# Two-block network on one core: gate projection inside the attention stage, semaphore clears outside a Block, and the first expert pieces loaded during routing

## The reference

```
h = rms_norm(x);  proj = h @ w_in          # 1024 x 7168
lru_in, lru_gate, q, k, v, g_lru, g_attn = split(proj)   # 7 parts of 1024 columns
y_lru  = (gelu(lru_gate) * rg_lru(conv(lru_in))) @ w_lru_o
y_attn = diff_attention(q, k, v) @ w_attn_o   # 8 heads, two maps each, causal by chunks of 64
x = x + (sigmoid(g_lru) * y_lru + sigmoid(g_attn) * y_attn) @ w_out
x = x + cross_attention(x, mem);  x = x + two_level_moe(rms_norm(x))
```

## Time and profile before

| | |
|---|---|
| median of 3 runs | 4880.08 us (4880.0 to 4886.49) |
| profiled execution | 4875.11 us, its span 4873.3 us |
| TensorE busy | 4016.8 us, 82% of the span |
| granted TensorE clock, mean | 0.906 |
| proj_g stage | about 3075 to 3262 us |
| attention stage | about 3267 to 3587 us |
| routing of the first expert layer | about 1754 to 1842 us |

### The profile page before, as it was taken

How to read it: one execution, slowest core, us unless ns; L and a number is a source line. 1 busy time by engine, 2 the same in 40 slices (tenths; PEclk the granted TensorE clock), 3 DMA queues, 4 the chain that set the end, 5 groups by cost and what they waited for, 6 DMA issues and landing times. The chain is left out here.

```text
span 4873.3 us, 76497 instructions
## 1 busy us (share of the span) xinstructions
PE 4016.8 (82%) x31217; PEld 3213.4 (66%) x31217; DVE 2769.6 (57%) x4050; ACT 2034.3 (42%) x3437; POOL 470.9 (10%) x376
## 2 busy tenths in 40 slices
PE   6999877868887747999859888777779896499994
PEld 4888654448886526888748666665668655288883
DVE  4222154666654667999741675216652445399995
ACT  3111023645443315777531444116641333277772
POOL 0000012210001200111010231000000000111111
PEclk8999977979998878999969999889989898699997
DMA  5332212652223418999642333231112313699996
GB/s 198 130 135 95 105 64 63 188 149 78 80 75 126 142 71 356 389 398 390 260 160 86 99 110 103 95 118 40 40 57 82 112 52 128 252 402 411 412 412 250
DMA packets 368225, 842.35 MB, mean 173 GB/s; under 512 B 32207, under 2 KB 241135, under 8 KB 317446
## 3 DMA queue, kind: packets, MB, share of 16 engines
q1 hardware_dynamic: 349790, 787.43, 43.8%
q0 software_dynamic: 12032, 41.96, 2.7%
q10 hardware_dynamic: 6056, 8.08, 0.5%
HBM read 673.03 MB, written 164.35 MB: 172 GB/s over the span
## 5 line engine op out<-in xcount | busy, mean ns | idle before, releaser
L504 PE MATMUL psum<-proj_hi,proj_w 128*128 128x512 f32 (+2 forms) x1728 | 462.0, 356 | 15.4 <-DVE proj_w L546 13.8
L2719 DVE TENSOR_TENSOR moe_lo<-moe_raw,moe_hi 128x2048 fp32r<-128x2048 f32 x192 | 436.4, 2288 | 45.2 <-ACT moe_hi L2667 45.1
L4346 DVE TENSOR_TENSOR moe_lo<-moe_raw,moe_hi 128x2048 fp32r<-128x2048 f32 x192 | 428.2, 2284 | 33.7 <-ACT moe_hi L4301 33.7
L2667 ACT ACTIVATE moe_hi<-moe_raw 128x2048 fp32r<-128x2048 f32 x192 | 367.8, 1919 | 136.9 <-PE psum L2620 136.8
L4301 ACT ACTIVATE moe_hi<-moe_raw 128x2048 fp32r<-128x2048 f32 x192 | 356.9, 1910 | 41.5 <-PE psum L4262 41.5
L504 PEld LDWEIGHTS psum<-proj_hi,proj_w 128*128 128x128 f32 (+1 forms) x1728 | 304.1, 188 | 69.0 <-DVE proj_w L546 14.2
L504 PE MATMUL psum<-proj_lo,proj_w 128*128 128x512 f32 (+2 forms) x864 | 306.4, 355 | 0.0
L515 DVE COPY proj_out<-psum 128x512 f32<-128x512 f32 (+3 forms) x54 | 32.5, 602 | 355.3 <-PE psum L504 355.3
L1796 DVE COPY_PREDICATED chunks_X<-chunks_msk,psum 128x128 f32<-128x128 int32 x400 | 107.8, 301 | 161.5 <-PE psum L1549 137.3
L1709 ACT ACTIVATE chunks_T<-psum 128x128 f32<-128x128 f32 x400 | 103.1, 277 | 216.0 <-PE psum L1539 211.0
L504 PE MATMUL psum<-h_hi,proj_g_w 128*128 128x512 f32 x512 | 159.9, 394 | 29.2 <-DVE proj_g_w L546 29.2
(11 more groups left out here) (634 smaller groups left out, 9690.1 us busy)
## 6 DMA issues: line engine op xcount, KB each, us to landing
moe_raw<-in_w_down SPq DMA_DIRECT2D x128, 1024.0 KB, 8.1
moe_raw<-in_w_gate_up SPq DMA_DIRECT2D x128, 1024.0 KB, 10.3
moe_raw<-in_w_gate SPq DMA_DIRECT2D x64, 1024.0 KB, 9.0
moe_raw<-in_w_up SPq DMA_DIRECT2D x64, 1024.0 KB, 10.0
uT<-proj_out SPq DMA_DIRECT2D x35, 640.0 KB, 3.0
chunks_pr<-prim SPq DMA_DIRECT2D x40, 512.0 KB, 4.1
proj_raw<-in_w_in SPq DMA_DIRECT2D x17, 1024.0 KB, 7.8
hT<-in_w_mod SPq DMA_DIRECT2D x32, 512.0 KB, 4.7
```

The costliest lines, as they stand in the source:

```text
L504: ins = nc.tensor.matmul(bank[e * nch + c][0:width, 0:n], l, r, start=(k == 0 and i == 0), stop=(k == KD - 1 and i == 2))
L2667: nc.scalar.activation(hi[:, n % R], raw[:, n % RAW], ACT.Copy).then_inc(s["hi_ready"], 1)
L2719: nc.vector.tensor_tensor(lo[:, n % R], raw[:, n % RAW], hi[:, n % R], ALU.subtract).then_inc(s["lo_ready"], 1)
L4346: nc.vector.tensor_tensor(lo[:, n % R], raw[:, n % RAW], hi[:, n % R], ALU.subtract).then_inc(s["lo_ready"], 1)
```

## The change

Three things change.

1. **Semaphore clears.** The exit of a Stage no longer opens a Block: GpSimd gets the clears directly after the stage's last barrier. The other engines go on. The semaphores stay reserved until the next exit.
2. **First pieces.** The eight ring slots of moe1 (four pieces of w_gate, four of w_up of expert 0) are loaded in route1, behind the router's weights and ahead of the clearing of acc. Their room is what mix's input took, and a new tile.
3. **Gates.** The stage proj_g and the stage branches are gone. The 768 gate matmuls become 32 units of 24, one in each wide step of attention: half of a unit ahead of turn(j-1), half behind it, into bank 7. ACT splits 16 weight tiles (gate_leading), DVE makes their rests (gate_rest), ACT empties each unit (gate_out), and SP loads 16 tiles of 512 KB and stores 32 results of 256 KB within attention. columns_of moves to bank 5 and to steps i = 0 to 3. gT is loaded in mixed, in eight DMAs of 512 KB, of which four stand ahead of the second weight tile. gemm_rows takes h_hi and h_lo as room for its weights, with the same instructions.

```diff
     def __exit__(self, *exc):
-        if exc[0] is None:
-            with self.nc.Block() as block:
-                @block.gpsimd
-                def _(pool):
-                    for s in self.sems:
-                        pool.sem_clear(s)
+        if self.sems:
+            if Stage.retired is not None:
+                Stage.retired.close()
+            for s in self.sems:
+                self.nc.gpsimd.sem_clear(s)
+            Stage.retired = self.sem_ctx
...
@@ route1, SP
                 sp.dma_start(wr[:, :, :], w_router.rearrange("(k p) e -> p k e", p=P)).then_inc(w_in, 16)
+                for n in range(ahead.RAW):
+                    sp.dma_start(ahead.raw(n), ahead.rows(w_gate if n < 4 else w_up, 0, n % 4)).then_inc(ahead.raw_in[n], 16)
                 sp.wait_ge(zeroed, 1)
...
@@ experts1, SP
                 def load(n, src):
-                    if n >= RAW:
-                        sp.wait_ge(s["lo_ready"], n - RAW + 1)
-                    sp.dma_start(raw[:, n % RAW], src).then_inc(raw_in[n % RAW], 16)
+                    if n < RAW:
+                        return
+                    sp.wait_ge(s["lo_ready"], n - RAW + 1)
+                    sp.dma_start(raw(n), src).then_inc(raw_in[n % RAW], 16)
...
@@ diff_attention
-        STATS, GROUPS_AT = PAIR + 2, PAIR + 4
+        STATS, GROUPS_AT = PAIR + 2, PAIR + NT
...
+                load_g(0)
+                load_g(1)
+                for u in range(2 * TILES_G):
+                    if u % 4 == 0 and 2 <= u // 4 + 1 < HEADS2:
+                        sp.wait_ge(s["o_mm"], NT * (u // 4))
+                        load(u // 4 + 1)
+                    if u % 2 == 0:
+                        load_g(u // 2 + 2)
+                    c, b = u // 2, u % 2
+                    sp.wait_ge(s["g_ev"], u + 1)
+                    sp.dma_start(gates[c * P:(c + 1) * P, b * BANK:(b + 1) * BANK], g_out[:, u % 4, :]).then_inc(g_stored[u % 4], 16)
...
+                def gate_unit(u, part):
+
+                    c, b = u // 2, u % 2
+                    if part == 0:
+                        pe.wait_ge(s["g_lo"], c + 1)
+                        if u:
+                            pe.wait_ge(s["g_ev"], u)
+                    for k in range(4 * part, 4 * part + 4):
+                        for i, (l, r) in enumerate(((0, 0), (1, 0), (0, 1))):
+                            ins = nc.tensor.matmul(bank[7][:, :], g_w[:, c % 2, l, k, :], h_part[r][:, k, b * BANK:(b + 1) * BANK],
+                                                   start=(k == 0 and i == 0), stop=(k == KD - 1 and i == 2))
+                    if part == 1:
+                        ins.then_inc(s["g_mm"], 1)
...
+                    u = unit_at(j)
+                    if u is not None:
+                        gate_unit(u, 0)
                     if 1 <= j <= J:
                         turn(j - 1)
+                    if u is not None:
+                        gate_unit(u, 1)
                     if 2 <= j <= J + 1:
                         values(j - 2)
...
@@ attention, ACT
+                def gate_leading(c):
+                    act.wait_ge(g_in[c % 2], 16 * (c // 2 + 1))
+                    if c >= 2:
+                        act.wait_ge(s["g_mm"], 2 * (c - 1))
+                    nc.scalar.activation(g_w[:, c % 2, 0, :, :], g_raw[:, c % 2], ACT.Copy).then_inc(s["g_hi"], 1)
+
+                def gate_out(u):
+                    act.wait_ge(s["g_mm"], u + 1)
+                    if u >= 4:
+                        act.wait_ge(g_stored[u % 4], 16 * (u // 4))
+                    nc.scalar.activation(g_out[:, u % 4, :], bank[7][:, :], ACT.Copy).then_inc(s["g_ev"], 1)
+
+                gate_leading(0)
                 act.wait_ge(s["lam"], 1)
...
@@ mixed_T
                 load(0)
-                load(1)
+                for k in range(KD):
+                    sp.dma_start(act_T[0][:, k, :], lru[k * P:(k + 1) * P, :]).then_inc(lru_in[k], 16)
+                    if k == 3:
+                        load(1)
```

More of the change, by code:

```diff
@@ L2431, in _, with __init__, raw, rows @@
                                 .then_inc(lo_ready, 1)
-def route1(nc, bank, cst, hT, w_router, acc, idx, gates):
+class Ahead1:
+    RAW = 8
+    def __init__(self, nc, hold, room):
+        self.first = room[:, :, :].rearrange("p (r k) n -> p r k n", k=2)
+        self.second = hold.enter_context(nc.sbuf_tensor("ahead1_raw", [P, self.RAW // 2, 2, D], F32))
+        self.raw_in = [nc.alloc_semaphore(f"ahead1_raw_in{i}") for i in range(self.RAW)]
+    def raw(self, n):
+        n, half = n % self.RAW, self.RAW // 2
+        return self.first[:, n] if n < half else self.second[:, n - half]
+    @staticmethod
+    def rows(m, e, j):
+        return m[e, 2 * j * P:2 * (j + 1) * P, :].rearrange("(p k) n -> p k n", k=2)
+def route1(nc, bank, cst, hT, w_router, acc, idx, gates, ahead, w_gate, w_up):
     with Stage(nc, "route1") as st:
@@ L2516, in _, with experts1 @@
                 nc.vector.tensor_copy(idx[:, E1:E1 + 1], bank[5][:, E1:E1 + 1]).then_inc(fin, 1)
[L2519 to L2525 removed]
+def experts1(nc, bank, cst, h2, w_gate, w_up, w_down, acc, idx, gates, xs_in, added, ahead, room):
+    RAW, R = ahead.RAW, 4
     with Stage(nc, "moe1") as st:
[L2527 removed]
+        raw, raw_in, rows = ahead.raw, ahead.raw_in, ahead.rows
+        xs, ye = room[:, 0, :], room[:, 1, :]
+        sg, hid = (room[:, 2 + n, :].rearrange("p (c n) -> p c n", c=2) for n in range(2))
         hi, lo = st.sb("hi", [P, R, 2, D], F32R), st.sb("lo", [P, R, 2, D], F32R)
[L2529 removed]
         xh, xl = st.sb("xh", [P, 2, KD, P], F32R), st.sb("xl", [P, 2, KD, P], F32R)
[L2531 removed]
         hT_hi, hT_lo = st.sb("hT_hi", [P, KD, P], F32R), st.sb("hT_lo", [P, KD, P], F32R)
[L2533 to L2534 removed]
         names = ("hi_ready", "lo_ready", "piece_mm", "x_tr", "xh_ready", "xl_ready", "sg_ready", "hid_ready", "h_tr",
@@ L3252, in pair_at, with unit_at @@
             return (n // PAIR, n % PAIR) if n >= 0 and n % PAIR < count and n // PAIR < J // PAIR else None
+        def unit_at(j):
+            return nb(j) if j < J and wide(j) else None
         with nc.Block() as block:
@@ L3304, in turn @@
                         pe.wait_ge(s["evB"], nb(j))
+                    if wide(j) and j > GROUPS_AT:
+                        pe.wait_ge(s["out"], 4 * ((j - GROUPS_AT) // PAIR + 1))
                     for t in range(i + 1):
@@ L3390, in _ @@
                         finished(*pair_at(j, GROUPS_AT, 4))
+                    u = unit_at(j)
+                    if u is not None:
+                        gate_out(u)
+                        if u % 2 == 0 and u // 2 + 1 < TILES_G:
+                            gate_leading(u // 2 + 1)
             @block.vector
@@ L3461, in _, with mixed_T @@
                         scale(*pair_at(j, STATS + 1, 2))
-def mixed_T(nc, bank, w_a, w_b, act_T, act_lo, a_in, gates, mT):
+                    u = unit_at(j - 1) if j else None
+                    if u is not None and u % 2 == 0 and u // 2 + 1 < TILES_G:
+                        gate_rest(u // 2 + 1)
+def mixed_T(nc, bank, w_a, w_b, lru, act_T, act_lo, act_hi, gates, mT):
     RAW, R = 2, 3
@@ L3471, in mixed_T @@
         w_hi, w_lo = st.sb("w_hi", [P, R, KD, P], F32R), st.sb("w_lo", [P, R, KD, P], F32R)
-        act_hi = st.sb("act_hi", [P, 2, KD, T], F32R)
+        lru_in = [st.sem(f"lru_in{k}") for k in range(KD)]
         g = st.sb("g", [P, 2, T])
@@ L4478, in program @@
                           h_rows=[mod[MOD_G2:MOD_G2 + 1, :], mod[MOD_S2:MOD_S2 + 1, :]], h_out=h2)
-                route1(nc, bank, cst, h2T, x["w_router"][0], acc, idx, gates)
-        experts1(nc, bank, cst, h2, x["w_gate"][0], x["w_up"][0], x["w_down"][0], acc, idx, gates, tokens_in, rows_added)
+                with ExitStack() as early:
+                    ahead = Ahead1(nc, early, lT)
+                    route1(nc, bank, cst, h2T, x["w_router"][0], acc, idx, gates, ahead, x["w_gate"][0], x["w_up"][0])
+                    experts1(nc, bank, cst, h2, x["w_gate"][0], x["w_up"][0], x["w_down"][0], acc, idx, gates, tokens_in, rows_added,
+                             ahead, h2T)
     second(nc, psum, bank, cst, col, tabs, x, scratch, x1, acc, mod[MOD_GT2:MOD_GT2 + 1, :], x2, out, stop)
```

124 lines of the change are left out of this document (71 added, 53 removed).

## The result

The changed kernel takes 4751.57 us (median of 4 runs, 4746.25 to 4758.52), the kernel before beside it 4880.04 (4 runs, 4867.44 to 4886.49): a ratio of 0.9749, 95% interval 0.9722 to 0.9775. A second measurement, with other runs of both, gave 4758.42 against 4870.16: 0.9767 (0.9753 to 0.978). The profiled execution of after took 4754.62 us with a span of 4752.7 us, 120.6 less than the span before.

The account below looks back on a forecast made before the run. TensorE, busy 82% of the span, was taken as the bound, with holes in attention's chain and waits at clearing seams. Terms -195.5 + 128.4 + 2 - 38 - 4 = -107.1 gave 4773 us; own range 4757 to 4792, 8 in 10: 4744 to 4808.

Parts of the forecast that it names:

- the likeliest case: Whole kernel: the forecast itself, 4773 us, own range 4757 to 4792, chance 0.62.
- the clock rises: Rival, attention: filled steps keep TensorE's clock high outside narrow ones, -20 us, so 4753 us; chance 0.15.
- Start of attention: proj_g's first DMA to attention's first exponential: 212.5 us removed, 17 in its place, -195.5 us.
- Attention: Attention itself: 174.1 us of gate matmuls, less 45.9 and 5.8 of holes filled, plus 6 for columns, +128.4 us.
- The holes filled: Attention: TensorE's waits that units fill, 45.9 us for exponentials and 5.8 at the heads' seams and the end.
- Units: Attention's wide steps: waiting for the predecessor's eviction just fits, 0 us, bound 6; splits and evictions hidden.
- Mixed: Start of mixed: gT lands while group 0 runs, group 1's operands some 2 us later, +2 us, bounds 0 and 8.
- Clears: Stage seams: GpSimd clears beside SP's DMA, except 5.6 us where GpSimd is first in the next stage, -38 us.
- Early pieces: Start of moe1: the gather without the 8 MB beside it takes 5.4 us instead of 9.4, -4 us.

Follow-up runs that it names:

- the kernel with the clears on TensorE and the later lambda: Changed kernel with first gate tile later, lambda chain behind first exponentials, clears on TensorE's queue; 4736.64 us (0.9737) against 4862.6.
- the dose: Changed kernel with 12, then 18, of the 24 matmuls of every gate unit left out; 4668.58 us (0.9581) and 4634.6 us (0.9523) against 4867.02.
- control: The changed kernel measured again, nothing else changed; 4758.42 us (0.9767) against 4870.16.
- experiment: Changed kernel with the first expert stage's first pieces loaded inside that stage, as before; 4755.64 us (0.9757) against 4870.16.

## Why the prediction was right, and where it was off

It said 4773 us, and 4751.57 were measured: inside the range, 21 us under the value, and 5 below the lower end of the likeliest case's own range. 13.5 us of that are in the spans (-120.6 for -107.1). The other 8: the profiled execution of before lay 5 us under its median, that of after 3 us above its own, which says nothing of the change. The total is nearer to the 4753 us of the rival "the clock rises" than to 4773, and that is chance: most of the difference is a clock that changed without the filled steps that the rival wants (9.5 us in attention), and the clears (3.4).

**Start of attention** (-195.5, measured -192.5). The mechanism is as described: the gate tile lands last and lambda's exponential stands behind it. The mis-sized term is the landing: 9.5 + 2.6 = 12.1 us after q's issue by the rate of addnorm's stretch, 15.4 in the trace. The work behind the landing took 4.6 us (4.8 in the sum). What I did not weigh is that the order itself is a choice: the tile is first used in step 4, and putting it behind the first steps gives 7.5 us of the stage.

**Attention** (+128.4, measured +118.9). The part on which most hung holds to 2 us, on the right ground. Against the kernel with the clears alone, whose clock is like that of after, the change adds 395.4 - 265.0 = 130.4 us from first to last exponential. That is made of wide steps from 19.62 to 35.05 us in seven heads and the last head's 12.2 (120.2 in all), columns and small waits in the narrow steps 6.0 (the columns' 1.3 in each of heads 3, 5 and 7 are 3.9, where 6 were forecast; 0.3 more in each of seven heads makes it up by luck), and 4.5 that I did not have: the wide steps of heads 2, 4 and 6, just behind the normalisation of a pair, took 36.4 to 36.6 us instead of 35.05. Head 2's wide steps in after, then in the kernel with the clears on TensorE and the later lambda:

```profile
3176.95:3213.52 36.57, 36.57 (x205) 29.23 (x203) 17.59 (x27) 16.81 (x39) 0.00 (x0) 0.97 0.11 36
...
3159.41:3194.67 35.26, 35.26 (x204) 28.25 (x202) 17.60 (x27) 16.81 (x39) 0.00 (x0) 1.00 0.12 38
```

The low stretch that begins in the narrow steps reached 2 us into them (0.97), and where it did not (1.00) they took 35.26: these 4.5 us are mostly the clock's. In the kernel with the clears alone the same steps were at 0.97 too and took 19.62, the hole covering it. The holes filled are some 49 us (8 x 6.2), forecast 51.7.

The mis-sized term is the clock, which the sum leaves out: the steps of the kernel before took 11.8 us more at the clock granted to them than with the clears alone. I had set this at nothing in the forecast and at -20 in the rival "the clock rises". The rival had the sign and the wrong cause. The 11.8 us go with the clears alone, and gate work added to that kernel's wide steps changes the low time little if at all (37, 33, 31 and 32 us); no run has gate work with the clears as they were, so what it would do there is open. The wide steps of head 5 were at 0.99 to 1.00 with or without units, so there was nothing to gain in them; only units in the narrow steps brought the low time down, to 18 us, at a price of 47. The rule of the Trainium skill, "TensorE: Matmul & The Clock Gate", "Part 1: The HAM clock gate", that activity releases the throttle, agrees with that last run, in which the narrow steps, where the throttle had stood, were filled; of the wide steps it promised more than the runs show.

**Units.** No wait for a predecessor's eviction (0.0 us), and splits and evictions hidden, as said; that this "just fits" is a matter of the wide steps, since in the narrow ones the same wait came to 20.6 us. Half of the units takes off half of their matmul time (86.4 of 174 us); the dose shows that TensorE alone sets the wide steps.

**Mixed** (+2, measured +0.5): the late operands of group 1 cost less than I took. The rule of the Trainium skill weighed there ("DMA: Bandwidth & Descriptors", "Bandwidth") would have had over +4. Here the trace differs from it: in 16 us of mixed's start, with these DMAs of 512 KB in flight, after moved 382 GB/s (3485 to 3501 us), and the stage grew by 0.5, which speaks for the row.

**Clears** (-38, measured -41.4; alone 44.0 in the seams). My discount of 5.6 us for seams at which GpSimd goes first was too large. Only at moe1's (1.2 us) did the runs show that the seam shrank and the work came no earlier.

**Early pieces** (-4, measured -4.9, or 4.2 between control and experiment): the gather fell to 4.7 us, 0.7 below the 5.4 taken and at the 4.8 of the bound.

**Open.** Why the low stretches of attention fall elsewhere once the clears are changed, or the columns moved, was not tried. With the clears alone the seam ahead of the stage is 1.7 us shorter, and everything ahead of it 40 us earlier.

## What to carry to other kernels

Work of a full engine is free in another stage only up to the hole that the chain leaves there (here 6.2 us in every 19.6): read chain length and busy time of one step at full clock, and price what is beyond the knee at its full duration. Look as well at what a piece of the new work waits for itself: in the narrow steps the units filled the holes and opened as many by waiting for the emptying of their bank. When a stage gets new operands, look at what stands ahead of its first result in each queue, and put there only what the first step uses. And compare a stage's length at equal granted clock, step by step, before a difference is put down to an edit: here 12 us in a stage that the edit hadn't touched came with another granted clock.

## What the runs showed of the hardware that was not expected

The same attention code ran 276.8 and 275.5 us in two profiles of one kernel, and 265.0 in a kernel that differs from it only in how semaphores are cleared; in the narrow steps at a granted clock of 0.88 four steps took 14.08 us, at 1.00 12.45, while DVE's and ACT's busy times were equal. Head 5's wide steps without units took 19.62 or 19.63 us at 0.99 or 1.00 in every kernel that has them. Without a block, a seam between stages costs 0.3 us where SP's load goes first and no store has to land, 0.7 to 3.0 us with one. A gather of 512 KB took 9.3 us from issue to use with 8 MB issued around it, and 4.7 us without them.
